# Products of probabilities and values as three rounded products of split operands, in the attention without sinks

## The chip, the core and the metric

The kernel runs on one core of a Trainium2 chip. Five engines work side by side and meet through semaphores: TensorE (PE; its weight loads are shown as PEld), VectorE (DVE), ScalarE (ACT), GpSimd (POOL) and SyncE (SP, which issues transfers). The metric is the device time of one launch in microseconds; three runs of the kernel before gave 2701.19 to 2704.44, median 2703.84.

## What is computed

The reference is one layer of a hybrid encoder over 512 prompt rows and 64 sample rows with 2048 features: a combined projection, two kinds of attention, an output projection, layer norms, a wide two-step network and a gated sum. Group B of the attention has 16 heads of 64 features, no sinks, and a forgetting term; for the prompt it is

```python
def fox_attention(q, k, v, f_q, f_k, pos_q, pos_k):
    s = jnp.einsum("bqhd,bkhd->bhqk", q, k, preferred_element_type=jnp.float32) * ATTN_SCALE
    s = s + jnp.swapaxes(f_q, 1, 2)[..., :, None] - jnp.swapaxes(f_k, 1, 2)[..., None, :]
    s = jnp.where(pos_k[None, :] <= pos_q[:, None], s, -jnp.inf)
    p = jax.nn.softmax(s, axis=-1)
    return jnp.einsum("bhqk,bkhd->bqhd", p.astype(v.dtype), v)
```

The change is about the last line: probabilities times values.

## The kernel before

**Layout.** Features lie on the 128 partitions, rows of the batch along the free axis (512 prompt and 64 sample columns, 576 in all, in two halves of 288). A product of the main stream (`products`, L614) is made of operands split into a rounded part and a rest (`w_hi`, `w_lo`, `x_hi`, `x_lo`): three products, each in two matmuls of 288 columns, added up in PSUM. One projection tile is 16 chunks of six such matmuls.

**Pairs and slots.** Group B has 8 pairs of heads. While TensorE computes the 3 x 16 = 48 chunks of the projections of pair q + 1 (values, keys, queries), it does the attention of pair q in between. `fox_between` is called ahead of each chunk c of the 48: at c = 2 it transposes the pair's values into `scores_ps` (L826, L827), at c = 5 it waits for all that the pair needs, and at c = 5, 8, 11, ... it calls `attend` with slot j = 0, 1, 2, ... 13 (`FOX_SLOTS`). A pair has 10 steps: steps 0 to 3 are the four query tiles of 128 prompt rows of the first head, 4 to 7 those of the second, 8 and 9 the sample rows of both. Query tile qt looks at qt + 1 key tiles of 128. In slot j TensorE does

- the scores of step j (L754, L755, and a mask added at L759) into `scores_ps`, in products of rounded operands,
- the transposes of the probabilities of step j - 3 (L787 for prompt steps, L790 for sample steps) into `turn_ps`,
- the products of the probabilities of step j - 4 with the values (L807) into `out_ps`.

So slot 4 has the products of step 0 (one key tile), slot 7 and slot 11 those of steps 3 and 7 (four key tiles). Before, values `fv` and transposed probabilities `f_pt` are plain 32-bit numbers; a product has 64 weight columns (one head) and is recorded as two matmuls.

**The other engines in a slot.** VectorE's `attend` takes the maximum of the scores of step j (L1575), then the reciprocal of the sum (L1580) and the scaling (L1583) of step j - 1. ScalarE's takes the exponential of step j (L1076) and copies the transposed probabilities of step j - 3 out of `turn_ps` into one of two places of `f_pt` (L1025). Between the slots VectorE and ScalarE split weights (`ahead.upto`, at every eighth chunk), and at c = 33 and 34, between slots 9 and 10, ScalarE takes the rounded parts of the next pair's keys and cached keys and VectorE their rests (`lows`, L1610), while GpSimd copies them to the other half of the partitions (L2104).

All engines run their instructions in the order of the code, so that a wait on one holds up all that stands behind it there. Every loop over pairs is a hardware loop of 3 rounds with two pairs in each, the seventh and eighth pair stand alone; the eighth runs beside the output projection (`LAST_SLOTS`).

Of the kernel before, what the change touches and what calls it, by code (L numbers as in the profile page):

```python
# [200 lines left out]
def build(nc, t):  # L201
# [5 lines left out]
    with outer:  # L207
# [3 lines left out]
        def sem(name):  # L211
            return outer.enter_context(nc.semaphore(name))
# [69 lines left out]
        fv = sb("fv", [128, 5, 128], f32, fox)  # L282
        c_v = sb("c_v", [128, 4, 128], f32, fox)
        f_p = sb("f_p", [128, 4, P_COLS], f32, fox)
        f_pt = sb("f_pt", [128, 2, 512], f32, fox)
        v_t = sb("v_t", [128, TOK], f32, fox)
        k_t = sb("k_t", [128, TOK], f32, fox)
# [20 lines left out]
        hr_1 = sb("hr_1", [128, TOK], f32, fast)  # L308
        fast.close()
        staged = (st[:, 0, :], st[:, 1, :])  # L310
        ops_d = nc.dram_tensor("ops_d", (JOBS, 2, FAST, 128, HALF), f32, kind="Internal").ap()
        h_saved_d = nc.dram_tensor("h_saved_d", (KT, 128, TOK), f32, kind="Internal").ap()
        hid_d = nc.dram_tensor("hid_d", (STD_UP, 128, TOK), f32, kind="Internal").ap()
# [46 lines left out]
        normed = sem("normed")  # L360
        turned = sem("turned")
        turn_out = sem("turn_out")
        weighed = sem("weighed")
        out_free = sem("out_free")
        v_turned, fv_ready = sem("v_turned"), sem("fv_ready")
# [242 lines left out]
        def _(pe):  # L608
# [126 lines left out]
            def attend(kind, j, pair, i=None, dp=0):  # L735
# [43 lines left out]
                if 3 <= j <= STEPS + 2:  # L779
                    s = j - 3  # L780
                    head, qt = step_of(s)
                    pe.wait_ge(normed, lin(g0 + s + 1, i, dg))
                    pe.wait_ge(turn_out, lin(g0 + s + 1, i, dg))
                    cols_ = key_cols(kind, head, qt)
                    for k, col in enumerate(cols_):
                        if qt < 4:
                            ins = nc.tensor.transpose(turn_ps[:, 128 * k:128 * k + 128], p[:, s % 4, col:col + 128], ident[:, :])  # L787
                        else:
                            keys = SAMPLE if k == len(cols_) - 1 else 128
                            ins = nc.tensor.transpose(turn_ps[0:keys, 64 * k:64 * k + 64], p[64:128, s % 4, col:col + keys],  # L790
                                                      ident[64:128, 64:128])
                    ins.then_inc(turned, 1)
                if j >= 4:
                    s = j - 4
                    head, qt = step_of(s)
                    pe.wait_ge(turn_out, lin(g0 + s + 2, i, dg))
                    if s == 8:
                        pe.wait_ge(exp_done, lin(g0 + STEPS + 2, i, dg))
                    if s == 8 and kind == "fox":
                        pe.wait_ge(cv_landed, lin(16 * (pair - PAIRS) + 16, i, 16 * dp))  # L800
                    width = 128 if qt < 4 else SAMPLE
                    dst = out_ps[64 * head:64 * head + 64, 128 * qt:128 * qt + 128] if qt < 4 else \
                        scores_ps[64 * head:64 * head + 64, 512 - SAMPLE:512]
                    vals = value_tiles(kind, qt)
                    for k, (vt, at) in enumerate(vals):
                        keys = SAMPLE if qt == 4 and k == len(vals) - 1 else 128
                        ins = nc.tensor.matmul(dst, vt[0:keys, at, 64 * head:64 * head + 64],  # L807
                                               pt[0:keys, s % 2, width * k:width * k + width],
                                               start=k == 0, stop=k == len(vals) - 1)
                    ins.then_inc(weighed, 1)  # L810
# [81 lines left out]
            def fox_between(c, q, i=None, dp=0, slots=FOX_SLOTS):  # L892

                pair = PAIRS + q
                if c == 2:
                    wait_freed(pe, T_FOX + 3 * q, i, 3 * dp)
                    pe.wait_ge(exp_done, lin(STEPS * pair + 2, i, STEPS * dp))
                    pe.wait_ge(out_free, lin(2 * pair + 1, i, 2 * dp))
                    turn_values(v_t).then_inc(v_turned, 1)
                if c == 5:  # L900
                    pe.wait_ge(fv_ready, lin(2 * q + 2, i, 2 * dp))
                    pe.wait_ge(op_dve, lin(OP_FOX_A + 6 * q + 6, i, 6 * dp))
                    pe.wait_ge(op_pool, lin(OP_FOX_P + 6 * q + 6, i, 6 * dp))
                    pe.wait_ge(forget_rows, lin(96 * q + 96, i, 96 * dp))
                    pe.wait_ge(zeroed_p, ZERO_ALL)
                for j in slots.get(c, ()):
                    attend("fox", j, pair, i, dp)

# [8 lines left out]
            for i in range(3):  # L917
                for j in range(2):
                    fox_tiles(1 + j, j, i, 2)
            fox_tiles(7, 6)  # L920


            wait_freed(pe, T_O - 2)
# [99 lines left out]
        def _(act):  # L1023
# [39 lines left out]
                if c % 2 == 1:  # L1063
                    ahead.upto(u + 1 + c // 2)

            def attend(kind, j, pair, i=None, dp=0):

                g0, dg = STEPS * pair, STEPS * dp
                p, pt = (s_p, s_pt) if kind == "swa" else (f_p, f_pt)
                if j < STEPS:  # L1070
                    head, qt = step_of(j)
                    act.wait_ge(negmax, lin(g0 + j + 1, i, dg))
                    act.wait_ge(turned, lin(g0 + 2 + max(0, j - 3), i, dg))
                    at, width = span(kind, j)
                    s = j % 3
                    nc.scalar.activation(p[:, j % 4, 0:width], scores_ps[:, at:at + width], ACT.Exp,  # L1076
                                         bias=stat[:, s, 0:1], scale=1.0, accum_out=stat[:, s, 1:2]).then_inc(exp_done, 1)
                if 3 <= j <= STEPS + 2:
                    s = j - 3
                    head, qt = step_of(s)  # L1080
                    act.wait_ge(turned, lin(g0 + s + 3, i, dg))
                    act.wait_ge(weighed, lin(g0 + s + 1, i, dg))
                    width = turn_width(kind, qt)
                    copy(pt[:, s % 2, 0:width], turn_ps[:, 0:width]).then_inc(turn_out, 1)
                if j in (12, 14):
                    act.wait_ge(weighed, lin(g0 + 2 + (8 if j == 12 else 10), i, dg))
                    kt = lin(pair, i, dp)
                    dst = feature_tile(acc, kt)
                    if j == 12:
                        copy(dst[:, 0:PROMPT], out_ps[:, :]).then_inc(out_free, 1)  # L1090
                    else:
                        copy(dst[:, PROMPT:TOK], scores_ps[:, 512 - SAMPLE:512]).then_inc(out_free, 1)
                        if kind == "swa" and pair < PAIRS - 1:
                            act.wait_ge(exp_done, lin(g0 + STEPS + 2, i, dg))
                            set_sinks(pair + 1, i, dp)
# [98 lines left out]
                copy(halves(fq1[0:64, 0, :]), ps[0:64], SCALE).then_inc(op_act, 1)  # L1194
                copy(halves(fq1[64:128, 1, :]), ps[64:128], SCALE).then_inc(op_act, 1)

            def fox_values(att, i=None, dp=0):
                act.wait_ge(v_turned, lin(att + 1, i, dp))
                copy(fv[:, 0:4, :], scores_ps[:, 0:512].rearrange("p (a b) -> p a b", a=4)).then_inc(fv_ready, 1)
                copy(fv[0:64, 4, :], scores_ps[0:64, 512:640]).then_inc(fv_ready, 1)  # L1200

            def fox_pair(q, att, i=None, dp=0):
                for c in range(3 * KT):
# [41 lines left out]
            for c in range(KT + 2):  # L1245
# [4 lines left out]
                if k >= 0:  # L1250
                    if k % 4 == 0:
                        ahead.upto(U_O + k // 4 + 2)
                    if k == 2:
                        fox_values(7)
                    for j in LAST_SLOTS.get(k, ()):
                        attend("fox", j, 2 * PAIRS - 1)
            attend("fox", SLOTS, 2 * PAIRS - 1)
            act.wait_ge(out_free, 1 + 4 * PAIRS)
            act.wait_ge(y_sum, KT)
# [214 lines left out]
        def _(dve):  # L1474
# [90 lines left out]
                        low(c - 1)  # L1565
                low(KT - 1)

            def attend(kind, j, pair, i=None, dp=0):

                g0, dg = STEPS * pair, STEPS * dp  # L1570
                p = s_p if kind == "swa" else f_p
# [4 lines left out]
                if 1 <= j <= STEPS:  # L1576
# [5 lines left out]
                    row = p[:, (j - 1) % 4, 0:width]  # L1582
                    V.tensor_scalar(row, row, stat[:, s, 2:3], None, ALU.mult)\  # L1583
                        .then_inc(normed, 1)

            dve.sem_inc(w_split, RING)
            dve.sem_inc(tile_free[0], 2)
# [132 lines left out]
            def fox_queries(att, i=None, dp=0):  # L1720
# [5 lines left out]
                dve.wait_ge(op_dve, lin(OP_FOX_A + 6 * att + 6, i, 6 * dp))  # L1726
                dve.sem_inc(tile_free[n % 2], 1)

            def fox_pair(q, att, i=None, dp=0):
                n0, dn, df = T_FOX + 3 * (q or 0), 3 * dp, 6 * dp  # L1730
                for c in range(3 * KT):
# [6 lines left out]
                    if att is not None:  # L1738
                        if c == 0:
                            fox_queries(att, i, dp)  # L1740
                        for j in FOX_SLOTS.get(c, ()):
                            attend("fox", j, PAIRS + att, i, dp)
                    if q is not None:
# [25 lines left out]
            for c in range(KT + 3):  # L1769
# [7 lines left out]
                if k >= 0:  # L1777
                    if k % 4 == 0:
                        ahead.upto(U_O + k // 4 + 2)
                    for j in LAST_SLOTS.get(k, ()):  # L1780
                        attend("fox", j, 2 * PAIRS - 1)
            operand_low(KT - 1)

            def residual(dst, n, i=None, dn=0):
# [291 lines left out]
        def _(pool):  # L2076
# [87 lines left out]
            def fox_pair(q, att, i=None, dp=0):  # L2164
# [26 lines left out]
                if q == 0:  # L2191
                    pool.wait_ge(out_free, 1 + 2 * PAIRS)
                    pool.wait_ge(weighed, 2 + STEPS * PAIRS)
                    zeros(ZERO_SWA + 4, other_halves(fq2))
                for dst, name in ((fq2, "rows_q"), (fk2, "rows_k"), (fc2, "rows_c")):
                    for head, at in ((0, 64), (1, 0)):
                        pool.dma_start(dst[at:at + 4, head, :].bitcast(f32),
# [196 lines left out]
```

## Time and profile before

| | |
|---|---|
| median of three runs | 2703.84 us |
| profiled execution, its own time | 2705.9 us |
| its span, first to last instruction | 2704.3 us |
| TensorE busy in the span | 98% |
| VectorE, ScalarE, GpSimd busy | 67%, 47%, 17% |
| mean granted TensorE clock | 0.994 |

The attention of the first seven pairs of group B lies between 356 and 747 us of the span, 55.81 us a pair. The page gives busy shares of the whole span; for a change in one stage the stretches and the order of time inside that stage count. In the timelines below a row is one instruction, or several of one kind in a row (x2), with the start and the length of all of them; matmul lengths include the way through the array, so the pace of a stream is the distance between starts.

### The profile page before, as it was taken

To read this page: it belongs to the slowest core of one execution; us is meant where nothing else is said; L and a number is where in the kernel's file an instruction comes from. 1 tells how busy PE (TensorE), PEld (TensorE's weight loads), DVE (VectorE), ACT (ScalarE), POOL (GpSimd) and SP (SyncE) were. 2 spreads that over 40 slices of the span, in tenths; PEclk is the share of its full clock that TensorE was granted. 3 is DMA by queue.
4 is the path that set the end of the run, shared out by engine and by line. 5 is a ranking of instruction groups with operands and counts; after the bars stand their busy time and mean duration, and the time that the engine had idled before them with its cause. 6 is when DMAs were issued, how large, how long until landed. Compare 5 with 4: busy or idle time off the path is not lost.

```text
span 2704.3 us, 50796 instructions
## 1 busy us (share of the span) xinstructions
PE 2651.4 (98%) x19581; PEld 2571.0 (95%) x19581; DVE 1808.0 (67%) x2898; ACT 1265.0 (47%) x2367; POOL 455.1 (17%) x726
## 2 busy tenths in 40 slices
PE   8899999999989999999999999899999999999998
PEld 6788899999979999999999999899999999999998
DVE  7754444434374466788888888788888888877632
ACT  4444443434342235566666666545454555425421
POOL 0110121112121111233333333210111010000000
PEclk9999999999999999999999999999999999999999
DMA  4111222222212224455555555874664453322331
GB/s 155 63 55 32 64 77 83 82 73 78 73 36 94 79 91 163 156 189 191 192 192 191 186 188 186 317 264 155 216 217 157 154 216 107 132 93 72 108 101 58
DMA packets 108284, 360.78 MB, mean 133 GB/s; under 512 B 17696, under 2 KB 25760, under 8 KB 107552
## 3 DMA queue, kind: packets, MB, share of 16 engines
q1 hardware_dynamic: 66880, 224.29, 25.4%
q0 software_dynamic: 39568, 132.23, 13.1%
q8 instruction: 156, 2.56, 0.4%
q10 hardware_dynamic: 1616, 1.18, 0.1%
q14 instruction: 64, 0.52, 0.1%
HBM read 282.59 MB, written 75.04 MB: 132 GB/s over the span
## 4 chain that ended last, share of the span: by engine, by line
PE 93%; DVE 3%; DMA 2%; ACT 1%; issue 1%; ACTq 0%; POOL 0%; DVEq 0%; POOLq 0%
PE tile L614 33%; PE misc L696 18%; PE misc L986 17%; PE tile L696 5%; PE tile L986 5%; PE tile L666 4%; PE misc L807 4%; PE misc L614 3%; DMA a_raw<-in_w 2%; PE misc L787 1%; PE misc L709 1%; PE misc L755 1%; PE misc L754 1%; DMA acc<-h_saved_d 0%; PE misc L759 0%
## 5 line engine op out<-in xcount | busy, mean ns | idle before, releaser
L614 PE MATMUL tile<-x_hi,w_hi 128*128 128x288 f32 (+1 forms) x2208 | 496.9, 307 | 10.6 <-DVE x_lo L1768 7.4
L614 PE MATMUL tile<-x_hi,w_lo 128*128 128x288 f32 (+1 forms) x2208 | 474.2, 296 | 0.0
L614 PE MATMUL tile<-x_lo,w_hi 128*128 128x288 f32 (+1 forms) x2208 | 473.7, 296 | 0.0
L614 PEld LDWEIGHTS tile<-x_hi,w_hi 128*128 128x128 f32 (+1 forms) x2208 | 351.0, 188 | 37.3 <-issue 28.8
L1025 ACT ACTIVATE a_lo<-a_raw 128x512 fp32r<-128x512 f32 (+1 forms) x420 | 273.9, 656 | 176.0 <-PE misc L986 89.2
L614 PEld LDWEIGHTS tile<-x_lo,w_hi 128*128 128x128 f32 (+1 forms) x2208 | 355.0, 188 | 1.1
L614 PEld LDWEIGHTS tile<-x_hi,w_lo 128*128 128x128 f32 (+1 forms) x2208 | 354.8, 188 | 1.2
L1482 DVE TENSOR_TENSOR w_lo<-w_raw,w_hi 128x1024 fp32r<-128x1024 f32 x170 | 223.0, 1330 | 132.1 <-ACT w_hi L1025 131.7
L696 PE MATMUL misc<-t_hi,a_lo 128*128 128x288 f32 x1008 | 256.0, 294 | 0.0
L1025 ACT ACTIVATE w_hi<-w_raw 128x1024 fp32r<-128x1024 f32 x170 | 177.3, 1053 | 160.8 <-PE tile L614 124.8
L1910 DVE TENSOR_TENSOR a_lo<-a_raw,a_lo 128x512 fp32r<-128x512 f32 x336 | 221.1, 685 | 0.7 <-ACT a_lo L1025 0.7
L986 PE MATMUL misc<-x_hi,a_lo 128*128 128x288 f32 x1344 | 196.3, 295 | 3.2 <-ACT st L1025 3.2
L986 PEld LDWEIGHTS misc<-x_hi,a_lo 128*128 128x128 f32 x1344 | 184.4, 188 | 3.4 <-DVE a_lo L1910 3.4
L1025 ACT ACTIVATE st<-misc 128x288 f32<-128x288 f32 x266 | 107.8, 405 | 160.3 <-PE misc L986 136.6
L1575 DVE TENSOR_REDUCE stat<-misc 128x1 f32<-128x257 f32 (+7 forms) x160 | 73.8, 462 | 162.1 <-PE misc L759 145.1
L986 PE MATMUL misc<-t_hi,a_lo 128*128 128x288 f32 x1120 | 175.2, 297 | 6.8 <-ACT st L1025 6.8
L696 PEld LDWEIGHTS misc<-t_hi,a_lo 128*128 128x128 f32 x1008 | 177.6, 188 | 0.0
L986 PEld LDWEIGHTS misc<-t_hi,a_lo 128*128 128x128 f32 x1120 | 158.9, 189 | 8.1 <-issue 8.0
L1899 DVE TENSOR_TENSOR a_raw<-a_raw 128x512 f32<-128x512 f32 x224 | 148.9, 685 | 25.1 <-DMA a_raw<-in_w 25.1
L1829 DVE TENSOR_TENSOR a_raw<-a_raw 128x1024 f32<-128x1024 f32 x112 | 136.4, 1218 | 0.2
L696 PE MATMUL misc<-x_hi,a_lo 128*128 128x288 f32 x448 | 131.2, 293 | 0.0
L1076 ACT ACTIVATE f_p<-misc,stat 128x128 f32<-128x128 f32 (+2 forms) x80 | 45.6, 571 | 173.1 <-DVE stat L1575 173.1
(303 smaller groups left out, 5972.4 us busy)
## 6 DMA issues: line engine op xcount, KB each, us to landing
a_raw<-in_w SPq DMA_DIRECT2D x224, 512.0 KB, 4.3
w_raw<-in_w SPq DMA_DIRECT2D x170, 512.0 KB, 3.5
ops_d<-st POOLq DMA_DIRECT2D x280, 144.0 KB, 3.7
ops_d<-hr POOLq DMA_DIRECT2D x112, 144.0 KB, 4.5
x_hi<-ops_d POOLq DMA_DIRECT2D x24, 576.0 KB, 7.1
x_lo<-ops_d POOLq DMA_DIRECT2D x24, 576.0 KB, 10.1
t_hi<-ops_d POOLq DMA_DIRECT2D x24, 576.0 KB, 12.7
a_lo<-ops_d POOLq DMA_DIRECT2D x9, 576.0 KB, 11.6
```

Source lines behind the costliest of these rows:

```text
L614: ins = nc.tensor.matmul(dst[:, h, :], w, x[:, h * HALF:(h + 1) * HALF], start=first and a == 0, stop=last and a == 2)
L666: ins = nc.tensor.matmul(tile_ps(n + j)[:, h, :], w[:, slot, cut], x[:, h, :], start=k == 0 and a == 0, stop=k == 3 and a == 2)
L696: ins = nc.tensor.matmul(banks[r], w, x[:, row + k, cols_], start=r in (0, 1, 3) and k == 0 and n == 0, stop=k == 7 and n == 2, skip_group ...
L807: ins = nc.tensor.matmul(dst, vt[0:keys, at, 64 * head:64 * head + 64], pt[0:keys, s % 2, width * k:width * k + width], start=k == 0, stop ...
L986: ins = nc.tensor.matmul(banks[r], w, x[:, k, :], start=r in (0, 1, 3) and k == 0 and m == 0, stop=k == 3 and m == 2, skip_group_check=r n ...
L1025: return nc.scalar.activation(out, in_, func, scale=scale)
L1076: nc.scalar.activation(p[:, j % 4, 0:width], scores_ps[:, at:at + width], ACT.Exp, bias=stat[:, s, 0:1], scale=1.0, accum_out=stat[:, s, 1 ...
L1482: V.tensor_tensor(w_lo[:, u % RING, :], w_raw[:, u % RING, :], w_hi[:, u % RING, :], ALU.subtract)\
L1575: V.reduce_max(stat[:, j % 3, 0:1], scores_ps[:, at:at + width], AX, negate=True).then_inc(negmax, 1)
L1829: V.tensor_tensor(raw(q, r), raw(q, first), raw(q, second), op).then_inc(sums, 1)
L1899: V.tensor_tensor(down_raw(d, r), down_raw(d, first), down_raw(d, second), op).then_inc(sums, 1)
L1910: V.tensor_tensor(down_lo(d, r), down_raw(d, r), down_hi(r), ALU.subtract).then_inc(a_ready, 1)
```

## The change

For the first seven pairs (not for the eighth, which runs beside the output projection) and the prompt steps:

- ScalarE copies the values twice more at c = 2: the two heads' values rounded into `fv_hi`, with 64 columns of zeros between the heads. VectorE takes the rests into `fv_lo` (`fox_values_low`), reading the transposed values from PSUM. TensorE waits for both at c = 5, ahead of the pair's first scores.
- ScalarE's copy of the transposed probabilities rounds them into `f_pt_hi`; VectorE takes the rest from `turn_ps` into `f_pt_lo`, at the end of its `attend` of the same slot, for steps 0 to 7. TensorE waits for that rest (`f_turn_lo`) ahead of the next step's transposes, which overwrite `turn_ps`, and ahead of the products.
- The products become three for each key tile (rounded values with rounded probabilities, rest of the values with rounded probabilities, rounded values with the rest of the probabilities), with 128 weight columns: one head's values and the zeros. They write all 128 partitions of `out_ps`, adding up from step 0's first product on.
- GpSimd fills the zeros once.

```diff
@@ tensor engine, attend @@
                     pe.wait_ge(turn_out, lin(g0 + s + 1, i, dg))
+                    if kind == "fox" and pair < 2 * PAIRS - 1 and 1 <= s <= 8:
+                        pe.wait_ge(f_turn_lo, lin(8 * (pair - PAIRS) + s, i, 8 * dp))
...
+                    if kind == "fox" and qt < 4 and i is not None:
+                        pe.wait_ge(f_turn_lo, lin(8 * (pair - PAIRS) + s + 1, i, 8 * dp))
+                        dst = out_ps[:, 128 * qt:128 * qt + 128]
+                        rounded_p, rest_p = f_pt_hi[:, s % 2, :], f_pt_lo[s % 2]
+                        for part, (v, p_) in enumerate(((fv_hi, rounded_p), (fv_lo, rounded_p), (fv_hi, rest_p))):
+                            for k in range(qt + 1):
+                                ins = nc.tensor.matmul(dst, v[:, k, 64 * head:64 * head + 128], p_[:, 128 * k:128 * k + 128],
+                                                       start=s == 0 and part == 0 and k == 0, stop=part == 2 and k == qt,
+                                                       skip_group_check=s > 0)
+                        ins.then_inc(weighed, 1)
+                        return
...
                     pe.wait_ge(fv_ready, lin(2 * q + 2, i, 2 * dp))
+                    if q < PAIRS - 1:
+                        pe.wait_ge(fv_split, lin(2 * q + 2, i, 2 * dp))
+                        pe.wait_ge(fv_lo_done, lin(2 * q + 2, i, 2 * dp))
@@ scalar engine, attend and fox_values @@
+                    if kind == "fox" and qt < 4 and not plain:
+                        act.wait_ge(weighed, lin(g0 + s + 1, i, dg))
+                        pt = f_pt_hi
                     copy(pt[:, s % 2, 0:width], turn_ps[:, 0:width]).then_inc(turn_out, 1)
...
+                if split_too:
+                    turned_values = scores_ps[:, 0:512].rearrange("p (a b) -> p a b", a=4)
+                    copy(fv_hi[:, :, 0:64], turned_values[:, :, 0:64]).then_inc(fv_split, 1)
+                    copy(fv_hi[:, :, 128:192], turned_values[:, :, 64:128]).then_inc(fv_split, 1)
@@ vector engine, attend @@
+                if kind == "fox" and not plain and 3 <= j <= 10:
+                    s = j - 3
+                    width = turn_width(kind, step_of(s)[1])
+                    dve.wait_ge(turn_out, lin(g0 + s + 2, i, dg))
+                    V.tensor_tensor(f_pt_lo[s % 2][:, 0:width], turn_ps[:, 0:width], f_pt_hi[:, s % 2, 0:width], ALU.subtract)\
+                        .then_inc(f_turn_lo, 1)
@@ vector engine, new at c == 2 of fox_pair @@
+            def fox_values_low(att, i=None, dp=0):
+                dve.wait_ge(fv_split, lin(2 * att + 2, i, 2 * dp))
+                turned_values = scores_ps[:, 0:512].rearrange("p (a b) -> p a b", a=4)
+                for h in range(2):
+                    own = slice(128 * h, 128 * h + 64)
+                    V.tensor_tensor(fv_lo[:, :, own], turned_values[:, :, 64 * h:64 * h + 64], fv_hi[:, :, own], ALU.subtract)\
+                        .then_inc(fv_lo_done, 1)
```

VectorE from the second rest of the cached keys (c = 34) through slot 10 (c = 35) to the next split of weights, before:

```order
L1610 SCALAR_TENSOR_TENSOR fc<-c_t,fc 64x512 [waits op_act]
L1578 REGISTER_ALU
L1580 RECIPROCAL stat<-stat 128x1 [waits exp_done]
L122 REGISTER_ALU
L1583 TENSOR_SCALAR f_p<-f_p,stat 128x576 [waits ch_dve]
L1481 REGISTER_ALU
L1482 TENSOR_TENSOR w_lo<-w_raw,w_hi 128x1024 [waits w_hi_done]
```

and after (`st_r` holds the rests, `misc` is PSUM with `turn_ps` in it):

```order
L1646 SCALAR_TENSOR_TENSOR fc<-c_t,fc 64x512 [waits op_act]
L1608 REGISTER_ALU
L1610 RECIPROCAL stat<-stat 128x1 [waits exp_done]
L122 REGISTER_ALU
L1613 TENSOR_SCALAR f_p<-f_p,stat 128x576 [waits ch_dve]
L1619 TENSOR_TENSOR st_r<-misc,f_pt_hi 128x512 [waits turn_out]
L1511 REGISTER_ALU
L1512 TENSOR_TENSOR w_lo<-w_raw,w_hi 128x1024 [waits w_hi_done]
```

The subtraction that makes the rest of step 7 now stands behind the scaling of step 9.

TensorE in slot 11 (c = 38), the transposes of step 8 and the products of step 7, before:

```order
L790 MATMUL misc<-ident_r,f_p 128x64 [waits turn_out,normed]
L790 MATMUL misc<-ident_r,f_p 128x64 x3
L790 MATMUL misc<-ident_r,f_p 64x64
L807 MATMUL misc<-f_pt,fv 64x128 [waits turn_out]
L807 MATMUL misc<-f_pt,fv 64x128 x3
```

and after (`st_r` holds the split values too):

```order
L799 MATMUL misc<-ident_r,f_p 128x64 [waits f_turn_lo,turn_out,normed]
L799 MATMUL misc<-ident_r,f_p 128x64 x3
L799 MATMUL misc<-ident_r,f_p 64x64
L820 MATMUL misc<-f_pt_hi,st_r 128x128 [waits f_turn_lo,turn_out]
L820 MATMUL misc<-f_pt_hi,st_r 128x128 x7
L820 MATMUL misc<-st_r 128x128 x4
```

The transposes wait for one semaphore more, and the four products of four key tiles have become twelve.

## Rows read from the trace of the kernel before

**Rows 1.** The page: busy times of the engines, and the chain by engine.

```profile
PE 2651.4 (98%) x19581; PEld 2571.0 (95%) x19581; DVE 1808.0 (67%) x2898; ACT 1265.0 (47%) x2367; POOL 455.1 (17%) x726
...
PE 93%; DVE 3%; DMA 2%; ACT 1%; issue 1%; ACTq 0%; POOL 0%; DVEq 0%; POOLq 0%
```

**Rows 2.** Windows: length, PE, PEld, DVE, ACT, POOL busy, PEclk, DMA, GB/s.

```profile
340.00:740.00 400.00, 400.00 (x2991) 373.29 (x2990) 163.62 (x299) 161.30 (x341) 73.39 (x117) 1.00 0.25 79
```

**Rows 3.** Timeline (start, length, us) of TensorE, slots 4 and 7, first pair.

```profile
367.72 0.40 PE L787 MATMUL misc<-ident_r,f_p 128*128 128x128 f32 x2
...
368.79 0.29 PE L614 MATMUL tile<-x_lo,w_hi 128*128 128x288 f32 x1
...
379.48 0.27 PE L787 MATMUL misc<-ident_r,f_p 128*128 128x128 f32 x1
...
381.07 0.29 PE L614 MATMUL tile<-x_lo,w_hi 128*128 128x288 f32 x1
```

**Rows 4.** Timeline of TensorE and its weight loads, slot 0, second pair.

```profile
411.94 0.19 PEld L755 LDWEIGHTS misc<-fk,fq 128*128 128x128 f32 x1
...
412.05 0.19 PEld L759 LDWEIGHTS misc<-tri_r,ident_r 128*128 128x128 f32 x1
...
412.16 0.30 PEld L614 LDWEIGHTS tile<-x_hi,w_hi 128*128 128x128 f32 x2
...
412.53 0.29 PE L614 MATMUL tile<-x_lo,w_hi 128*128 128x288 f32 x1
```

**Rows 5.** Timeline of TensorE, slot 11, first pair.

```profile
395.31 0.51 PE L790 MATMUL misc<-ident_r,f_p 64*128 64x64 f32 x5
395.75 1.09 PE L807 MATMUL misc<-f_pt,fv 128*64 128x128 f32 x8
...
397.14 0.29 PE L614 MATMUL tile<-x_lo,w_hi 128*128 128x288 f32 x1
```

**Rows 6.** Timeline of VectorE, the scaling of step 9, first pair.

```profile
395.37 0.56 DVE L1583 TENSOR_SCALAR f_p<-f_p,stat 128x576 f32<-128x576 f32 x1
```

**Rows 7.** Timeline, slot 11's transposes and the scaling of step 9, seventh pair.

```profile
730.19 0.51 PE L790 MATMUL misc<-ident_r,f_p 64*128 64x64 f32 x5
...
730.64 0.56 DVE L1583 TENSOR_SCALAR f_p<-f_p,stat 128x576 f32<-128x576 f32 x1
```

**Rows 8.** Groups by form on VectorE, 355 to 740: busy us, mean ns, idle.

```profile
L1575 DVE TENSOR_REDUCE stat<-misc 128x1 f32<-128x512 f32 x14 | 9.7, 692 | 16.4 <-PE misc L759 16.4
...
L1610 DVE SCALAR_TENSOR_TENSOR fq<-tile,fq 64x576 fp32r<-64x576 f32 x12 | 9.1, 755 | 8.4 <-ACT fq L1025 8.2
...
L1575 DVE TENSOR_REDUCE stat<-misc 128x1 f32<-128x256 f32 x14 | 5.9, 421 | 11.1 <-PE misc L759 11.1
```

**Rows 9.** Timeline of the eighth pair: TensorE wakes after ScalarE's copy.

```profile
773.59 0.37 ACT L1025 ACTIVATE f_pt<-misc 128x256 f32<-128x256 f32 x1
...
774.11 0.30 PE L787 MATMUL misc<-ident_r,f_p 128*128 128x128 f32 x1 [1.35 <-ACT f_pt L1025]
```

**Rows 10.** Timeline of chunks 2 to 5, second pair.

```profile
409.74 0.75 ACT L1025 ACTIVATE fv<-misc 128x512 f32<-128x512 f32 x2 [0.83 <-PE misc L827]
...
411.94 0.22 PE L754 MATMUL misc<-fk,fq 128*128 128x128 f32 x1
...
411.99 0.28 PE L755 MATMUL misc<-fk,fq 128*128 128x128 f32 x1
```

**Rows 11.** Windows as in rows 2, beside the eighth pair.

```profile
760.00:765.00 5.00, 2.92 (x18) 2.68 (x18) 4.74 (x9) 1.48 (x5) 2.20 (x2) 0.89 0.34 105
765.00:768.00 3.00, 3.00 (x16) 2.92 (x16) 2.79 (x6) 1.24 (x3) 0.67 (x1) 0.61 0.00 0
770.00:777.00 7.00, 5.65 (x41) 4.85 (x40) 6.13 (x11) 3.89 (x10) 1.34 (x2) 1.00 0.23 75
```

**Rows 12.** Timeline of TensorE, eighth pair, idle time before the row in brackets.

```profile
763.67 0.50 PE L754 MATMUL misc<-fk,fq 128*128 128x384 f32 x1 [2.08 <-ACT f_p L1076]
```

More of the change, by code:

```diff
@@ L284, in build @@
         f_p = sb("f_p", [128, 4, P_COLS], f32, fox)
+        own = ExitStack()
+        f_pt_hi = sb("f_pt_hi", [128, 2, 512], f32r, own)
+        own.close()
         f_pt = sb("f_pt", [128, 2, 512], f32, fox)
@@ L310, in build @@
         staged = (st[:, 0, :], st[:, 1, :])
+        st_flat = st_r[:, :, :].rearrange("p a b -> p (a b)")
+        fv_hi, fv_lo = (st_flat[:, 768 * k:768 * k + 768].rearrange("p (a b) -> p a b", a=4) for k in range(2))
+        f_pt_lo = (st_flat[:, 1536:1920], st_flat[:, 1920:2432])
         ops_d = nc.dram_tensor("ops_d", (JOBS, 2, FAST, 128, HALF), f32, kind="Internal").ap()
@@ L362, in build @@
         turn_out = sem("turn_out")
+        f_turn_lo, fv_split, fv_lo_done = sem("f_turn_lo"), sem("fv_split"), sem("fv_lo_done")
         weighed = sem("weighed")
@@ L904, in fox_between @@
                     pe.wait_ge(forget_rows, lin(96 * q + 96, i, 96 * dp))
-                    pe.wait_ge(zeroed_p, ZERO_ALL)
+                    pe.wait_ge(zeroed_p, ZERO_ALL + 2)
                 for j in slots.get(c, ()):
@@ L919, in _ @@
                     fox_tiles(1 + j, j, i, 2)
-            fox_tiles(7, 6)
+            fox_tiles(7, 6, 0)
             wait_freed(pe, T_O - 2)
@@ L1064, in ln_apply, with attend @@
                     ahead.upto(u + 1 + c // 2)
-            def attend(kind, j, pair, i=None, dp=0):
+            def attend(kind, j, pair, i=None, dp=0, plain=False):
                 g0, dg = STEPS * pair, STEPS * dp
@@ L1195, in fox_queries, with fox_values @@
                 copy(halves(fq1[64:128, 1, :]), ps[64:128], SCALE).then_inc(op_act, 1)
-            def fox_values(att, i=None, dp=0):
+            def fox_values(att, i=None, dp=0, split_too=True):
                 act.wait_ge(v_turned, lin(att + 1, i, dp))
@@ L1253, in _ @@
                     if k == 2:
-                        fox_values(7)
+                        fox_values(7, split_too=False)
                     for j in LAST_SLOTS.get(k, ()):
-                        attend("fox", j, 2 * PAIRS - 1)
+                        attend("fox", j, 2 * PAIRS - 1, plain=True)
             attend("fox", SLOTS, 2 * PAIRS - 1)
@@ L1566, in ln_apply, with attend @@
                 low(KT - 1)
-            def attend(kind, j, pair, i=None, dp=0):
+            def attend(kind, j, pair, i=None, dp=0, plain=False):
                 g0, dg = STEPS * pair, STEPS * dp
@@ L1740, in fox_pair @@
                             fox_queries(att, i, dp)
+                        if c == 2:
+                            fox_values_low(att, i, dp)
                         for j in FOX_SLOTS.get(c, ()):
@@ L1780, in _ @@
                     for j in LAST_SLOTS.get(k, ()):
-                        attend("fox", j, 2 * PAIRS - 1)
+                        attend("fox", j, 2 * PAIRS - 1, plain=True)
             operand_low(KT - 1)
@@ L2193, in fox_pair @@
                     pool.wait_ge(weighed, 2 + STEPS * PAIRS)
-                    zeros(ZERO_SWA + 4, other_halves(fq2))
+                    zeros(ZERO_SWA + 4, (*other_halves(fq2), fv_hi[:, :, 64:128].bitcast(f32), fv_lo[:, :, 64:128].bitcast(f32)))
                 for dst, name in ((fq2, "rows_q"), (fk2, "rows_k"), (fc2, "rows_c")):
```

## The prediction

> **What bounds the kernel now.** I read the page's shares first, then the stretch that the change touches, then single slots of it in order of time. TensorE is busy 98% of the span, and the chain that ended last is TensorE for 93% [rows 1]. In the attention without sinks (340 to 740 us) it is busy for all of 400.00 us at full clock, VectorE and ScalarE for 164 and 161 [rows 2]. So a microsecond saved or added in TensorE's own stream moves the end by as much. Work on VectorE or ScalarE is free until TensorE has to wait for it, and a wait in one place undoes what TensorE saved in the slots before it.
>
> **Shorter and longer blocks on TensorE.** A slot's blocks stand between products of the main stream, so I measure from the first transpose to the third main product behind the block. Before, with one key tile (two transposes, two product records), that is 368.79 - 367.72 = 1.07 us; with four key tiles (one transpose) it is 381.07 - 379.48 = 1.59 [rows 3]. After, every product loads 128 columns and streams 128. Rows of that form are the scores: successive loads of 128 rounded columns start 0.11 apart, and from the first main load behind them to the third main product takes 412.53 - 412.16 = 0.37 [rows 4]. The load, not the stream, sets that pace. With t transposes of 0.11 and 3n products the new length is 0.11 (t - 1) + 0.33 n + 0.37: 0.81 for n = 1, t = 2 and 1.69 for n = 4, t = 1. So the block gets 0.26 shorter with one key tile and 0.10 longer with four. Per key tile that is 0.12 more, so n = 2 and 3 give -0.14 and -0.02. The gain comes from the two turn-rounds between 128-wide and 64-wide work, which the wider weights make needless; the products themselves cost more (0.33 for 0.22 per key tile).
> Slots 4 to 7 (first head) sum to -0.32 per pair, -2.2 us over seven pairs. Slot 11 is different: its transposes are 64 rows high, so a turn-round before the products stays. From 395.75 I put twelve loads of 0.11 and 0.37, 397.44 for 397.14 [rows 5]: +0.30, or +0.16 if the first load can start 0.14 earlier. I take 0.30, 2.1 us in all. Slots 8 to 10 would save 0.42 per pair, but see the next part.
>
> **The new wait in slot 11.** Its transposes (step 8) now also wait until VectorE has taken the rest of step 7, since that rest is read from the same PSUM bank. VectorE does this last in slot 10, behind the four low halves of keys and cached keys and the reciprocal and scaling of step 9. In the first pair that scaling ends at 395.37 + 0.56 = 395.93 [rows 6], and the transposes began at 395.31 [rows 5]: VectorE is 0.62 late before the new subtraction has begun. In the last pair it is 731.20 against 730.19, 1.01 late [rows 7]. These are the first and the last of seven; in order they are 0.62, 0.68, 0.28, 0.35, 0.63, 0.69 and 1.01, 4.26 together. The subtraction reads 512 columns from PSUM; the nearest row is the maximum over 512 columns of PSUM, 0.69 [rows 8]. Successive VectorE instructions without a dependence overlap by some 0.08, so 0.61 more. Then TensorE has to wake: the one stall of this form runs from the end of ScalarE's copy at 773.96 to the transpose at 774.11, 0.15 [rows 9]. The stall is 4.26 + 7 x 0.76 = 9.6 us. The bounds for the subtraction: 0.54, which is 512 elements at the 1.06 ns each by which the maxima over 512 and 256 columns differ ((692 - 421) / 256), and 0.75, the low half of a query from PSUM [rows 8], so 8.5 to 10.0.
> That end is fixed by VectorE's and ScalarE's chain from slot 8's scores on, not by TensorE. So the 0.42 saved in slots 8 to 10 only makes TensorE wait longer, and counts nothing. The stall itself is hidden nowhere: behind the waiting transposes stand slot 11's products and then the main stream of the same tile. VectorE's new waits for ScalarE's copies hold up only the next slot's maximum and a split of weights that is due two units later, and VectorE has idle time for that in every other slot; in those, the rest of a step ends before the next slot's transposes.
>
> **Splitting the values.** At chunk 2 the values are transposed, at chunk 5 the first scores of the pair overwrite them. Now ScalarE's two rounded copies and VectorE's two rests must be done first. ScalarE's two copies of today end at 409.74 + 0.75 = 410.49 [rows 10]. Two more of 256 columns at 0.37 [rows 9] overlap by about 0.1 each: 411.1. Two rests at 0.42 [rows 8] give 411.9, and 0.15 to wake 412.05 to 412.1, against 411.94 now [rows 10]: 0.15 to 0.25 late, I take 0.2, 1.4 us for seven pairs. Bounds: nothing if the copies overlap more, 0.5 per pair if reading 4 runs of 64 is slower. The two zero fills on GpSimd happen once, ahead of the first pair, on an engine that is busy for 73 of these 400 us [rows 2], and cost nothing; if they were late, the first pair's first scores would wait.
>
> **Sum.** -2.2 + 2.1 + 9.6 + 1.4 = +10.9 us. Against the profiled execution (span 2704.3, its own time 2705.9) that is 2716.8; it lay 2.1 above the median of the three runs, 2703.84, so 2714.7 by the median. A measurement of this kernel can tell about 0.2%, 5.4 us, from no change.
>
> **Rivals.**
> 1. The wait in slot 11 is no wait. If VectorE had its rest ready by 395.3, slots 8 to 10 would keep their 0.42 per pair: -2.2 - 2.9 + 2.1 + 1.4 = -1.6, 2702.2, not slower. It decides from the point where the scaling of step 9 ends 0.76 before the transposes; the trace has it 0.28 to 1.01 behind them in all seven pairs [rows 5 to 7], and the order of the changed kernel puts the subtraction behind it. Only a VectorE that catches up there, for instance by not meeting GpSimd's casts in the low halves, speaks for it.
> 2. The loads are not the pace. The stream of 128 columns alone takes 0.05 to 0.06 (411.94 to 411.99, the load having been made ahead) [rows 10]. At 0.06 the 294 products of slots 4 to 7 and 11 (14 key tiles, three products, seven pairs) would cost 0.05 less each, 14.7 us: 2700.0, within 0.2%. The rows speak against it: the loads of scores, mask and the first main product stand 0.11 apart [rows 4].
> The Trainium skill (TensorE: Matmul & The Clock Gate, Back-to-back issue gap) gives about 81 ns per matmul for a stream of load and product pairs with 128 columns; by that the sum would be 8.5 us less, an estimate of 2706. No row here shows that pace for rounded 32-bit operands, so I leave it to this rival.
> 3. Both 1 and 2: all 420 products 0.05 cheaper on top of 2702.2, 2681, faster.
> 4. The clock falls. TensorE would stand still in slot 11 for the stall and the 0.42 it arrives early, 1.5 to 2.2 us. After an idle time of 2.08 [rows 12] the granted clock was 0.89 and 0.61 in two stretches around and behind it [rows 11], that is partly at 1.2 GHz in place of 2.4; after one of 1.35 [rows 9] it stayed 1.00 [rows 11]. The fall cost 0.11 x 5 + 0.39 x 3 = 1.7 us. In the last pair, with the longest wait, it may well come, 2716.4; in all seven it would be +12, 2726.6.
>
> **How the numbers follow.** Forecast, with one fall of the clock or none: 0.73, 2714.7, its own range 2711 to 2719 (stall 8.5 to 10.0, values 0 to 3.5, slot 11 1.1 to 2.1, one fall). Rival 1: 0.07. Rival 2: 0.05. Rival 3: 0.02. Rival 4 with three falls or more: 0.11, from 2720 to 2727. Something that no row shows: 0.02, put to slower. The range leaves out rivals 1 and 3, half of rival 2 and the upper half of rival 4: 2706 to 2724. Faster is rival 3, 0.02. Within 0.2% are rivals 1 and 2, and 0.05 of the forecast for two terms that come out low together, 0.17. Slower has the rest, 0.81.
>
> **What would show it.** After the change, the waits of TensorE in this stretch, none before, should list seven of 1.4 to 2.1 us at the 64-row transposes, ended by VectorE's subtraction, and seven of a few tenths at the first score of a pair. Seven pairs should each take about 1.5 us longer than 55.81. Blocks with one key tile should be 0.26 shorter, those with four 0.10 longer, with loads 0.11 apart. It would be wrong if the slot 11 transposes start without a wait, if the loads come closer than 0.11, or if the rests of other slots also end behind the next transposes, which would add up to 0.5 us in each.

## The result, and the profile after

The changed kernel ("after" in what follows, against "before") took 2727.99 us (median of four runs, 2721.26 to 2730.27), the kernel before, run beside it, 2704.14 (four runs, 2701.19 to 2705.53). The ratio is 1.0084 with the 95% interval [1.0072, 1.0096]: 23.9 us slower. The forecast of 2714.7 had the direction; the time lies 9 us above the forecast's own range (2711 to 2719) and 4 above the whole range (2706 to 2724), near where rival 4 had put seven falls of the clock (2726.6).

The profiled execution took 2728.65 us, 22.75 more than that of before, at a mean granted clock of 0.989 (before 0.994). The page of after, busy times and chain by engine, answers to [rows 1]:

```profile
PE 2665.3 (98%) x19721; PEld 2600.8 (95%) x19721; DVE 1839.4 (67%) x2968; ACT 1269.2 (47%) x2381; POOL 456.1 (17%) x728
...
PE 90%; DVE 4%; ACT 2%; DMA 2%; issue 1%; ACTq 0%; DVEq 0%; POOL 0%; POOLq 0%
```

It says little: TensorE is still busy for 98% of the span. The windows of the attention say more (columns as in [rows 2]; the first line answers to that row, the others are single stretches):

```profile
340.00:740.00 400.00, 390.93 (x2980) 381.33 (x2980) 185.97 (x356) 157.13 (x341) 66.41 (x106) 0.97 0.24 75
399.20:402.60 3.40, 3.40 (x16) 3.12 (x15) 0.87 (x1) 0.00 (x0) 0.00 (x0) 0.50 0.38 113
...
460.60:573.30 112.70, 110.07 (x863) 107.08 (x863) 52.56 (x103) 45.84 (x100) 19.76 (x32) 1.00 0.24 77
573.30:576.70 3.40, 3.40 (x16) 3.40 (x16) 1.23 (x1) 0.36 (x1) 0.00 (x0) 0.50 0.18 40
...
631.30:638.10 6.80, 6.80 (x31) 6.52 (x31) 1.23 (x1) 1.26 (x2) 0.00 (x0) 0.50 0.26 80
```

TensorE lacks 9 us of its 400, where it lacked none, and the granted clock is 0.97. That mean hides what happens: full clock for most of a pair, and stretches at 0.50, that is 1.2 GHz, with TensorE busy in all of them. The waits of TensorE between 340 and 780 us (line waited for, releaser, us in total, times, longest) name the new wait:

```profile
PE misc L799 <- DVE st_r L1619: 11.0, 7, 2.0
```

and the timeline of slot 11 in the first pair (start, length, idle time before in brackets; [rows 5, 6] are its rows of before) shows how it comes about:

```profile
395.47 0.56 DVE L1613 TENSOR_SCALAR f_p<-f_p,stat 128x576 f32<-128x576 f32 x1
...
395.95 0.67 DVE L1619 TENSOR_TENSOR st_r<-misc,f_pt_hi 128x512 fp32r<-128x512 f32 x1
...
396.77 0.48 PE L799 MATMUL misc<-ident_r,f_p 64*128 64x64 f32 x5 [1.57 <-DVE st_r L1619]
397.18 0.97 PEld L820 LDWEIGHTS misc<-f_pt_hi,st_r 128*128 128x128 f32 x8
...
398.07 0.53 PEld L820 LDWEIGHTS misc<-st_r 128*128 128x128 f32 x4
```

VectorE's scaling of step 9 ends at 396.03, its rest of step 7 at 396.62, and the transposes begin 0.15 later. The first low stretch of the clock (399.20) starts 2.4 us after TensorE is at work again.

**The seven pairs as a ledger.** A pair's length is the distance between its values being turned and the next pair's; before it is 55.81, after it is 58.94 in the first pair:

```profile
353.19 0.60 PE L826 MATMUL misc<-ident_r,v_t 128*128 128x128 f32 x4
...
409.00 0.38 PE L826 MATMUL misc<-ident_r,v_t 128*128 128x128 f32 x2
```

```profile
353.30 0.49 PE L846 MATMUL misc<-ident_r,v_t 128*128 128x128 f32 x3
...
412.24 0.60 PE L846 MATMUL misc<-ident_r,v_t 128*128 128x128 f32 x4
```

The table gives, for each pair, TensorE's idle time in slot 11, the length of the stretch at 0.50 that follows (a low stretch), and how much longer the pair is, to about 0.01. Three kernels of the experiments below stand beside it: e3 and e5 have the wait with the products of before, e6 has the products of after.

| pair | after: idle, low, longer | e3: idle, low, longer | e5: idle, low, longer | e6: idle, low, longer |
|---|---|---|---|---|
| 1 | 1.57, 3.4, 3.13 | 1.30, 0, 1.33 | 1.63, 3.4, 3.20 | 1.36, 3.4, 3.14 |
| 2 | 1.65, 3.4, 3.23 | 1.35, 0, 1.39 | 1.68, 3.4, 3.27 | 1.44, 3.4, 3.30 |
| 3 | 1.27, 0, 1.31 | 0.96, 0, 1.00 | 1.28, 0, 1.32 | 1.06, 0, 1.34 |
| 4 | 1.35, 3.4, 2.89 | 1.03, 0, 1.07 | 1.35, 0, 1.39 | 1.14, 3.4, 2.98 |
| 5 | 1.57, 6.8, 4.67 | 1.31, 0, 1.34 | 1.64, 3.4, 3.16 | 1.36, 0, 1.61 |
| 6 | 1.65, 3.4, 3.25 | 1.36, 0, 1.39 | 1.69, 0, 1.72 | 1.44, 6.8, 4.75 |
| 7 | 1.95, 6.8, 3.88 | 1.99, 3.4, 3.40 | 2.01, 3.4, 3.30 | 1.74, 3.4, 3.56 |

In the first six rows it balances: a pair without a low stretch is longer by its idle time and some 0.04 (e6: by 0.25 to 0.28, with one product that it adds), one with a stretch of 3.4 us by 1.5 to 1.6 more, one with 6.8 by 3.1. In the seventh the kernel before has a low stretch of its own, at a wait of 5.60 us that all these kernels have. So of after's 22.4 us, idle time and work make about 11.3 (11.0 idle, and 0.04 per pair, as in the third pair, which has no low stretch), and the rest, some 11, is the clock.

### The profile page after: what moved, and what is told of

The parts are those of the page before. It is cut to its first block, busy times and chain, and to the rows that moved or that the text cites. A ratio compares the mean times of both kernels' runs of the same rounds, so it can differ in the third digit from the quotient of the medians.

```text
span 2727.0 us, 51231 instructions
## 1 busy us (share of the span) xinstructions
PE 2665.3 (98%) x19721; PEld 2600.8 (95%) x19721; DVE 1839.4 (67%) x2968; ACT 1269.2 (47%) x2381; POOL 456.1 (17%) x728
## 4 chain that ended last, share of the span: by engine, by line
PE 90%; DVE 4%; ACT 2%; DMA 2%; issue 1%; ACTq 0%; DVEq 0%; POOL 0%; POOLq 0%
PE tile L621 31%; PE misc L703 18%; PE misc L1009 17%; PE tile L703 5%; PE tile L1009 5%; PE tile L673 4%; PE misc L621 3%; PE misc L827 2%; PE misc L820 1%; DMA a_raw<-in_w 1%; PE misc L716 1%; PE misc L796 1%; PE misc L762 1%; PE misc L761 1%; DVE stat L1605 1%
```

## The experiments

**e1: VectorE in time, the products as changed.** VectorE's rests of the cached keys are moved from c = 34 to c = 36, behind slot 10.

```diff
-                        if c == 34:
+                        if c == 36:
                             lows([(fc2[0:64, 0, :], c_t[0:64, :], fc1[0:64, 0, :], 1.0),
...
```

> The changed kernel with one edit: VectorE takes the two rests of the next pair's cached keys at chunk 36, behind slot 10's work, and no longer at chunk 34, ahead of it. So the rest of step 7 is ready before slot 11's transposes. Theory A (of the 22.7 us lost, 11 are the wait in slot 11, some 12 the clock that falls after it, and the blocks and the values nearly cancel): no wait in slot 11, no fall of the clock between 356 and 740, and 2702 to 2706 us, level with the kernel before. Rival B (the clock falls because the new products wait for their weight loads, twelve in a row): the wait goes, but the falls stay, some 3.4 us each in five or six pairs, 2711 to 2716.

2703.88 us (11 runs) against 2704.05 (21 runs): 0.9998 [0.9989, 1.0007]. Its timeline at slots 10 and 11, and its window as in [rows 2]:

```profile
391.12 0.61 DVE L1613 TENSOR_SCALAR f_p<-f_p,stat 128x576 f32<-128x576 f32 x1
391.98 0.69 DVE L1619 TENSOR_TENSOR st_r<-misc,f_pt_hi 128x512 fp32r<-128x512 f32 x1 [0.25 <-ACT f_pt_hi L1048]
392.59 1.99 DVE L1646 SCALAR_TENSOR_TENSOR fc<-c_t,fc 64x512 fp32r<-64x512 f32 x2
...
392.92 0.51 PE L799 MATMUL misc<-ident_r,f_p 64*128 64x64 f32 x5
```

```profile
340.00:740.00 400.00, 400.00 (x3131) 389.82 (x3130) 193.71 (x368) 163.15 (x352) 70.77 (x115) 1.00 0.24 78
```

The rest of step 7 is done at 392.67, the transposes follow at 392.92 without a wait, the clock stays at 1.00 and every pair is back at 55.80 to 55.84. So the whole loss comes from the place of that one subtraction in VectorE's queue: the idle time and all falls of the clock go with it. The three products alone neither slow TensorE down as a sum nor bring the clock down. This is the case of rival 1, priced at -1.6 us; in it the change gains nothing that can be measured (-0.2 us, interval -3.0 to +1.9).

**e2: the wait filled.** After, with seven products (twice recorded, into columns that nothing reads) ahead of slot 11's transposes.

```diff
+                    if kind == "fox" and pair < 2 * PAIRS - 1 and s == 8:
+                        pe.wait_ge(exp_done, lin(g0 + STEPS + 2, i, dg))
+                        for _ in range(7):
+                            nc.tensor.matmul(scores_ps[:, 512:640], mean_w[:, :], mean_w[:, :], start=True, stop=True)
                     pe.wait_ge(normed, lin(g0 + s + 1, i, dg))
```

> The changed kernel, and ahead of slot 11's transposes TensorE makes 7 plain 128-column products that nobody reads (0.22 us each, 1.5 us), which takes up the time in which it waits for VectorE. The wait is paid all the same, but the array is not idle. Theory A (an idle array lets the clock fall): no fall between 356 and 740, and some 2714 us, what the sum without the clock gave. Rival B (the load-paced products let it fall): the falls stay, 2722 or more. That the fill is longer than the wait in some pairs may cost up to 1 us in all.

2716.91 us (5 runs), 1.0050 [1.0036, 1.0064]. The timeline of its slot 11 in the first pair, and its window:

```profile
393.57 1.72 PE L792 MATMUL misc<-mean_w 128*128 128x128 f32 x14
395.31 0.48 PE L803 MATMUL misc<-ident_r,f_p 64*128 64x64 f32 x5
```

```profile
340.00:740.00 400.00, 399.75 (x3133) 390.40 (x3132) 193.17 (x367) 161.20 (x348) 72.48 (x116) 1.00 0.24 77
```

The same delay, spent working instead of standing: no pair is longer by more than 1.7 us (1.56 to 1.70, 11.4 in all), and the clock stays at 1.00 in this stretch. The expected 2714 was still 2.9 too low. It is 11 us faster than after (medians of two chips), about what the ledger puts to the clock. So here products that are thrown away cost less than standing still.

**e3: the wait alone, the products of before.** The kernel before, with VectorE's subtraction (its result unused) and TensorE's wait for it.

```diff
@@ tensor engine, ahead of the transposes @@
+                    if kind == "fox" and pair < 2 * PAIRS - 1 and 1 <= s <= 8:
+                        pe.wait_ge(f_turn_lo, lin(8 * (pair - PAIRS) + s, i, 8 * dp))
@@ vector engine, end of attend @@
...
+                    V.tensor_tensor(f_pt_lo[s % 2][:, 0:width], turn_ps[:, 0:width], f_pt[:, s % 2, 0:width], ALU.subtract)\
+                        .then_inc(f_turn_lo, 1)
```

> The kernel before with its plain products, and only the wait added: VectorE subtracts the transposed probabilities from their copy at the end of each of its slots 3 to 10 (nobody uses the result), and TensorE waits for that ahead of the next step's transposes. The wait in slot 11 alone: seven stalls of 1.0 to 1.8 us, 9.3 in all. Theory A (the idle time alone lets the clock fall): falls in some pairs as well, 1.7 us of loss each, 2716 to 2724. Theory C (it takes the idle time and the load-paced products behind it together): no falls, 2712 to 2715.

2713.98 us (5 runs), 1.0041 [1.0027, 1.0054]. TensorE's waits, then windows:

```profile
PE misc L795 <- DVE st_r L1594: 9.3, 7, 2.0
```

```profile
340.00:738.90 398.90, 389.61 (x2906) 363.48 (x2905) 188.17 (x353) 157.39 (x335) 72.10 (x116) 1.00 0.24 77
739.00:742.30 3.30, 3.30 (x15) 2.97 (x14) 1.23 (x1) 1.22 (x2) 0.00 (x0) 0.50 0.00 0
```

The wait is real and costs its own length, 9.3 us, and one fall behind the longest, 1.99. But the idle times of the first six pairs are also shorter than after's by 0.3, since nothing was saved in slots 8 to 10, so the run doesn't tell whether the shorter wait or the plain products kept the clock up. Two more runs, on another chip (before: 2703.87, 15 runs), bear on it.

**e5: e3 with idle times as long as after's.** One more unused subtraction of 256 columns in slot 10.

```diff
                     dve.wait_ge(turn_out, lin(g0 + s + 2, i, dg))
+                    if j == 10:
+                        V.tensor_tensor(st_flat[:, 0:256], turn_ps[:, 0:256], f_pt[:, s % 2, 0:256], ALU.subtract)
```

> The run with the wait alone and the plain products, its wait in slot 11 made longer by one more VectorE subtraction of 256 columns (0.34 us) whose result nobody uses. The idle times should then be 1.3 to 1.7 us and 2.3 in the last pair, those of the changed kernel, and the products behind them the plain ones. If the length of the idle time alone decides, the clock falls in four or five pairs as in the changed kernel: 2714 + 2.4 + some 8 = 2722 to 2727. If it takes the load-paced products as well, no falls but in the last pair: 2716 to 2718.

2721.98 us (4 runs), 1.0062 [1.0046, 1.0077]. Slot 11's transposes in the first and fourth pair, and the windows behind the first:

```profile
396.71 0.49 PE L795 MATMUL misc<-ident_r,f_p 64*128 64x64 f32 x5 [1.63 <-DVE st_r L1596]
...
571.66 0.49 PE L795 MATMUL misc<-ident_r,f_p 64*128 64x64 f32 x5 [1.35 <-DVE st_r L1596]
```

```profile
398.30:401.70 3.40, 3.40 (x15) 3.40 (x16) 1.23 (x1) 0.45 (x1) 0.00 (x0) 0.50 0.20 33
401.70:456.30 54.60, 52.92 (x397) 49.23 (x396) 25.56 (x50) 21.05 (x47) 9.88 (x16) 1.00 0.24 78
```

With plain products the clock falls too, when the idle times are longer: behind 1.63, 1.68, 1.64 and 2.01, not behind 1.28 and 1.35, nor behind 1.69 in the sixth pair. The median is 8.0 us above e3's, of which the longer idle times (11.3 for 9.3 in all) make 2.0. So the length of the idle time matters, and the split products aren't needed for a fall.

**e6: after with idle times as short as e3's.** e2 with one product in place of seven.

```diff
-                        for _ in range(7):
+                        for _ in range(1):
```

> The changed kernel with one plain product (two records, 0.22 us) ahead of slot 11's transposes in place of seven: the wait is the same, the idle time 0.2 to 0.3 shorter, 1.0 to 1.4 us, and the load-paced products stay behind it. If the length of the idle time decides, no falls but perhaps in the last pair, 2715 to 2718. If the load-paced products behind a shorter idle time are enough, falls in several pairs: 2721 to 2728.

2721.63 us (4 runs), 1.0061 [1.0046, 1.0076]. Slot 11's transposes in the fourth and fifth pair, and the windows behind the fourth:

```profile
569.50 0.49 PE L803 MATMUL misc<-ident_r,f_p 64*128 64x64 f32 x5 [1.14 <-DVE st_r L1623]
...
628.50 0.49 PE L803 MATMUL misc<-ident_r,f_p 64*128 64x64 f32 x5 [1.36 <-DVE st_r L1623]
```

```profile
570.90:574.20 3.30, 3.30 (x16) 3.30 (x15) 1.23 (x1) 0.65 (x1) 0.00 (x0) 0.50 0.12 20
574.30:686.90 112.60, 109.80 (x861) 106.89 (x861) 53.17 (x103) 45.14 (x99) 19.66 (x32) 1.00 0.23 77
```

Here the clock falls behind 1.14, 1.36, twice behind 1.44 and behind 1.74, and stays up behind 1.06 and a second 1.36. Of the idle times up to 1.36 with split products behind them (e6 and after) three of six brought a fall; with the plain products of e3 and e5 none of eight did. The medians agree: e6 is 7.7 us above e3, and idle time and work together (0.34 more in the third pair, where neither has a low stretch) make only some 2.4 of that. This points to the work behind the idle time as a second condition, but doesn't prove it: e6's idle times are also 0.05 to 0.11 longer than e3's in the first six pairs, they come at other moments, and no run changed the moment alone. Nor does a single length part falls from none: the same 1.36 goes both ways inside one execution. The four executions of after differ too, 2721.26 us at a mean clock of 0.993 for the fastest, 2727.34 to 2730.27 at 0.989 to 0.990 for the others.

**e4: split products only where they are shorter.** After with the three products for one and two key tiles (steps 0, 1, 4, 5) and the plain ones for three and four; the prompt steps 2, 3, 6 and 7 are then computed as before. Step 7 has no rest, so nothing waits in slot 11.

```diff
+SPLIT_STEPS = (0, 1, 4, 5)
...
@@ tensor engine @@
-                    if kind == "fox" and qt < 4 and i is not None:
+                    if kind == "fox" and s in SPLIT_STEPS and i is not None:
...
@@ vector engine @@
-                if kind == "fox" and not plain and 3 <= j <= 10:
+                if kind == "fox" and not plain and j - 3 in SPLIT_STEPS:
```

> The changed kernel, but only the steps with one or two key tiles (0, 1, 4 and 5) use three split products; steps 2, 3, 6 and 7 use the plain products of before, need no rest, and so slot 11 has no wait. By the lengths of the changed kernel's trace: slots 4 and 8 save 0.22 us, slots 5 and 9 0.09 to 0.11, the values cost 0.17 per pair: -0.47 per pair, -3.3 us, 2701 us, and no fall of the clock. If rival B holds (load-paced products alone let the clock fall), fewer of them in a row should still keep it up, so this run says little on it.

2698.80 us (11 runs), 0.9984 [0.9975, 0.9993], 5.2 us below the median of before (4.3 by the ratio), so faster than both the kernel before and the changed one. Two successive pairs' turned values stand 55.32 apart:

```profile
351.98 0.38 PE L856 MATMUL misc<-ident_r,v_t 128*128 128x128 f32 x2
...
407.30 0.27 PE L856 MATMUL misc<-ident_r,v_t 128*128 128x128 f32 x1
```

That is 0.49 less than before in each pair (expected 0.47), some 3.5 us over seven; the median moved by more, within its interval [-6.8, -1.9].

**e7: the values' wait taken away.** e4, with the turned values in the second bank of `scores_ps`, so that the first scores needn't wait for the rests; TensorE waits for these at c = 8. ScalarE's two copies into `fv` also change places.

```diff
-                    turn_values(v_t).then_inc(v_turned, 1)
+                    turn_values(v_t, 512 if q < PAIRS - 1 else 0).then_inc(v_turned, 1)
...
@@ c == 5 @@
-                        pe.wait_ge(fv_split, lin(2 * q + 2, i, 2 * dp))
-                        pe.wait_ge(fv_lo_done, lin(2 * q + 2, i, 2 * dp))
...
+                if c == 8 and q < PAIRS - 1:
+                    pe.wait_ge(fv_split, lin(2 * q + 2, i, 2 * dp))
+                    pe.wait_ge(fv_lo_done, lin(2 * q + 2, i, 2 * dp))
```

> The kernel with split products for one and two key tiles only, and the transposed values put into the other bank of the scores, so that only the second slot's scores (chunk 8) wait for the rests of the values. The wait at chunk 5 should go, 0.17 us a pair, 1.2 us in all: some 2698 us against 2699 of that kernel, 2704 of before; nothing else should move.

```profile
351.20 0.27 PE L856 MATMUL misc<-ident_r,v_t 128*128 128x128 f32 x1
...
406.34 0.27 PE L856 MATMUL misc<-ident_r,v_t 128*128 128x128 f32 x1
```

A pair now takes 55.15 by its turned values (55.14 in these two rows), 0.17 less than e4's: that is what the wait for the split values costs. The time, 2699.13 (11 runs, 0.9983 [0.9974, 0.9992]), can't show these 1.2 us beside e4, which ran on another chip.

## Why the prediction was right in its sum and wrong in its time

**Slots 4 to 7.** Predicted per slot -0.26, -0.14, -0.02, +0.10; measured, the same in all seven pairs to about 0.01, -0.22, -0.09, 0.00, +0.12 (the distance of the third main products around the slot). Rows of after that answer to [rows 3], first transpose and third main product in slots 4 and 7:

```profile
368.03 0.40 PE L796 MATMUL misc<-ident_r,f_p 128*128 128x128 f32 x2
...
368.88 0.43 PE L621 MATMUL tile<-x_lo,w_hi 128*128 128x288 f32 x2
...
379.47 0.28 PE L796 MATMUL misc<-ident_r,f_p 128*128 128x128 f32 x1
...
381.19 0.42 PE L621 MATMUL tile<-x_lo,w_hi 128*128 128x288 f32 x2
```

0.85 for 1.07 with one key tile, 1.72 for 1.59 with four. The loads do stand 0.11 apart, as the eight from 397.18 to 398.07 in slot 11 above show; rivals 2 and 3 fall. But each block is 0.02 to 0.05 longer than predicted, whatever its size, so the term is -1.3 us where -2.2 was predicted.

The Trainium skill (TensorE: Matmul & The Clock Gate, Back-to-back issue gap) would have put such a pair of load and product at 81 ns; for these operands the trace has 111 (0.89 / 8).

**Slot 11's products.** +0.32 per pair in e1, where no wait blurs it, 0.28 behind the wait in after's third pair (1.31 longer, of which 1.02 before the transposes); predicted 0.30.

**The wait in slot 11.** The mechanism, its place, its seven times and its parts were right: from the end of the scaling to the transposes 0.74 in the first pair (396.03 to 396.77), predicted 0.76. The idle time is 11.0 us in all, part of it time that TensorE had saved in slots 8 to 10: 0.31 per pair, predicted 0.42, eaten by the wait as predicted. What the forecast priced is how much later the transposes start within the pair than before: 1.35, 1.39, 1.02, 1.10, 1.31, 1.41 and 1.73, 9.3 in all. Slots 4 to 7 and the values (below) have a share of -0.02 per pair in these, so the wait is 9.4 for 9.6.

**The values at c = 5.** 0.17 per pair, predicted 0.2. The chain in the second pair was the predicted one, two copies, two rests, waking:

```profile
413.63 0.64 ACT L1048 ACTIVATE st_r<-misc 128x256 fp32r<-128x256 f32 x2
414.31 0.76 DVE L1770 TENSOR_TENSOR st_r<-misc,st_r 128x256 fp32r<-128x256 f32 x2 [1.25 <-ACT st_r L1048]
...
415.27 0.30 PE L761 MATMUL misc<-fk,fq 128*128 128x128 f32 x1
```

The expected seven entries of a few tenths don't show among the waits; they show as slot 0 being 0.17 longer and, in e7, as 0.17 less.

**Sum.** With slot 11 as in the third pair, -1.3 + 2.0 + 9.4 + 1.2 = 11.3 against the predicted 10.9. That it is so near is in part luck: the 0.9 by which slots 4 to 7 saved less than predicted is half made up by three terms that came out a little low. Without the falls of the clock the time would have been some 2715, within the forecast.

**The step that failed** is the clock: the chance of rival 4, 0.11, and with it the forecast "with one fall of the clock or none", which left the clock out of the sum. In its place the runs showed falls in six of the seven pairs, two of them of double length, some 11 us together (the ledger; after and e2 differ by 11.1). The rival's mechanism and its price were right: 1.5 to 1.6 us for a stretch of 3.4 us where 1.7 was predicted, 12 us for seven falls where some 11 came. Its chance was not. It rested on two idle times of the eighth pair, 2.08 with a fall [rows 11, 12] and 1.35 without [rows 9, 11]. The stalls that the prediction itself worked out, 1.5 to 2.2 us in rival 4 (1.4 to 2.1 among its signs), began above the second and reached past the first; nothing in those rows favoured "none". Nor does one case without a fall make 1.35 safe: in after's fourth pair the clock fell behind just that. The change became slower not by the products that it was about but by 11 us of waiting for VectorE, and about as much again for the clock that fell behind the waits.

**What stays open.** What decides whether the clock falls behind a given idle time. Length has a part in it (e3 and e5), but the same length goes both ways, in e6 and in the last section. Whether the split products add to it is not shown; e1 only shows that they don't do it without an idle time. Nor was a wait moved in time with all else kept. How the falls are spread over executions rests on one profile of each kernel and on the times and mean clocks of the others.

## What to carry to other kernels

A wait of a microsecond or two on TensorE has two prices: its own length, and a stretch at half the clock behind it that cost as much again here; where a sum contains such a wait several times, the falls belong in the forecast, and one or two rows without a fall don't take them out: the same wait went both ways here. When an engine off the critical path gets one more instruction that TensorE needs, look at what stands ahead of it in the queue: here moving two unrelated instructions behind it (e1) took away the whole loss. And split a change by size: a slot gained 0.22 us with one key tile and lost 0.12 with four, and the kernels with the gaining half alone (e4, e7) were the ones faster than before.

## What the runs showed of the hardware

- **The clock fell behind idle times of 1.14 to 2.01 us, though not behind each.** In slot 11 of these four kernels it fell behind every idle time from 1.44 up but one (1.69 in e5), behind three of eleven from 1.14 to 1.36, and behind none of the three below; the granted clock then is 0.50 for 3.4 or 6.8 us while TensorE is busy throughout. The Trainium skill (TensorE: Matmul & The Clock Gate, Why this matters for your kernels) asks only that idle times stay under about 3 us; in this kernel that is not enough.
- **A longer idle time need not bring a fall.** At the first scores of the eighth pair the clock fell behind 2.08 in before [rows 11, 12] and behind 1.95 in e1; it stayed at 1.00 behind 2.46 in e2 and behind 2.97 in e7. The row of e7, and the window behind it:

```profile
757.02 0.44 PE L769 MATMUL misc<-fk,fq 128*128 128x384 f32 x1 [2.97 <-ACT f_p L1109]
```

```profile
757.10:763.00 5.90, 4.76 (x34) 4.53 (x34) 5.62 (x13) 3.15 (x10) 1.34 (x2) 1.00 0.04 15
```

- **The same wait need not give the same clock.** Beside the output projection all nine kernels have a wait of 1.82 us for VectorE's `x_lo`, with the products of the main stream behind it. At it the clock fell in six (after, e2, e3, e4, e5, e7) and stayed up in three (before, e1, e6). The window of before, then that of after, each with the first 5.9 us behind the wait:

```profile
798.80:805.60 6.80, 5.80 (x38) 5.35 (x39) 3.27 (x5) 0.02 (x1) 1.19 (x2) 1.00 0.01 2
```

```profile
822.50:829.20 6.70, 5.88 (x24) 5.88 (x25) 2.27 (x3) 0.00 (x0) 1.18 (x2) 0.50 0.00 0
```

In after the clock is already down 0.8 us before that wait ends (at 823.32); in slot 11 the low stretches start 0.3 to 2.4 us behind the end of the wait.
- **Working costs less than standing.** In e2 the same delay, filled with products that nothing reads, left the clock at 1.00 between 340 and 740 us.
